# Normed frames for the gate and up projections: six of eight tiles into buffers of their own, written during the output projection

## The reference

```python
for l in range(DEPTH):                                   # DEPTH = 2
    hp = hp + mixer(rms_norm(hp, norm_mix[l]), w_in[l], ...) @ w_out[l]
    hp = hp + conv_ffn(rms_norm(hp, norm_ffn[l]), ...)

def rms_norm(x, g):
    return x * rsqrt(mean(x * x, axis=-1) + EPS) * g

def conv_ffn(h, prev, w_gate, w_up, conv_w, conv_b, w_down):
    g = h @ w_gate                                       # 1024 -> 2816
    u = h @ w_up                                         # 1024 -> 2816
    gp = concatenate([prev, g])                          # two rows of history
    gc = conv_b + sum(conv_w[i] * gp[i:i + l] for i in range(3))
    return (gelu(gc) * u) @ w_down                       # 2816 -> 1024
```

## Time and profile before

| | |
|---|---|
| median of 3 runs | 1730.74 us (1730.06 to 1736.03) |
| the profiled execution | 1730.43 us |
| its span in the trace | 1728.9 us |
| PE busy | 1640.0 us, 95% of the span |
| DVE, ACT, POOL busy | 815.6, 541.6, 374.4 us |
| mean granted TensorE clock | 0.97 of full speed |

### The profile page before, as it was taken

One profiled execution on the slowest core, in us unless ns is written; L12 is line 12 of the kernel. 1 busy time (PEld: TensorE's weight loads), 2 busy tenths in 40 slices (PEclk: granted clock), 3 DMA queues, 4 the chain that ended last, 5 costly groups with the idle time before them and its releaser, 6 DMA issues.

```text
span 1728.9 us, 30885 instructions
## 1 busy us (share of the span) xinstructions
PE 1640.0 (95%) x11500; PEld 1586.3 (92%) x11500; DVE 815.6 (47%) x1116; ACT 541.6 (31%) x829; POOL 374.4 (22%) x405
## 2 busy tenths in 40 slices
PE   5999988999999999999989998889999999999997
PEld 4999866898999999999989997579999999999997
DVE  6332378546454225553243325774554442455523
ACT  2221224514545113332132221353245531233311
POOL 5080010051222002222304501002422210122221
PEclk9999978999999999999999999799999999999998
DMA  4222343022232223322222213511223322233222
GB/s 163 68 69 74 115 171 130 2 79 85 97 121 89 97 87 104 121 70 71 81 82 65 71 61 135 211 59 38 66 87 130 120 88 73 85 122 101 69 77 85
DMA packets 44849, 160.77 MB, mean 93 GB/s; under 512 B 5952, under 2 KB 8416, under 8 KB 43936
## 3 DMA queue, kind: packets, MB, share of 16 engines
q1 hardware_dynamic: 40896, 129.11, 23.5%
q0 software_dynamic: 2464, 28.26, 4.1%
q10 hardware_dynamic: 1408, 2.30, 0.4%
HBM read 147.64 MB, written 30.88 MB: 103 GB/s over the span
## 4 chain that ended last, share of the span: by engine, by line
PE 70%; DVE 9%; issue 9%; ACT 6%; POOL 2%; DMA 2%; DVEq 1%; ACTq 1%; POOLq 0%; SPq 0%; PEldq 0%
PE PSUM L1312 55%; PE PSUM L1349 8%; PE PSUM L1298 4%; ACT WH L634 1%; PE PSUM L1340 1%; DVE CT L1230 1%; DVE CT L1233 1%; POOL YT L602 1%; ACT CT L787 1%; ACT CT L785 1%; DVE XNL L831 1%; DVE GP L1223 1%; DMA CAK<-ca_kt 1%; DVE RS L824 1%; DMA X<-x_in 1%
## 5 line engine op out<-in xcount | busy, mean ns | idle before, releaser
L1312 PE MATMUL PSUM<-XNH,WH 128*128 128x320 f32 x2400 | 557.1, 313 | 35.7 <-DVE XNL L831 32.6
L1312 PE MATMUL PSUM<-XNL,WH 128*128 128x320 f32 x2400 | 550.7, 311 | 0.0
L1312 PE MATMUL PSUM<-XNH,WL 128*128 128x320 f32 x2400 | 550.3, 310 | 0.0
L819 DVE TENSOR_TENSOR WL<-RAW,WH 128x1024 fp32r<-128x1024 f32 (+2 forms) x214 | 289.8, 1355 | 393.5 <-ACT WH L634 388.2
L1312 PEld LDWEIGHTS PSUM<-XNH,WH 128*128 128x128 f32 x2400 | 402.6, 189 | 41.7 <-DVE XNL L831 36.3
L634 ACT ACTIVATE WH<-RAW 128x1024 fp32r<-128x1024 f32 (+2 forms) x214 | 210.9, 987 | 636.3 <-PE PSUM L1312 586.0
L1312 PEld LDWEIGHTS PSUM<-XNH,WL 128*128 128x128 f32 x2400 | 404.7, 189 | 0.0
L1312 PEld LDWEIGHTS PSUM<-XNL,WH 128*128 128x128 f32 x2400 | 404.3, 189 | 0.0
L1312 PE MATMUL PSUM<-YH,WH 128*128 128x320 f32 x544 | 124.8, 311 | 5.1 <-DVE YL L1241 5.1
L1312 PE MATMUL PSUM<-YL,WH 128*128 128x320 f32 x544 | 124.6, 310 | 0.0
L1312 PE MATMUL PSUM<-YH,WL 128*128 128x320 f32 x544 | 124.5, 310 | 0.0
(11 more groups left out here) (196 smaller groups left out, 1747.3 us busy)
## 6 DMA issues: line engine op xcount, KB each, us to landing
RAW<-w_gu SPq DMA_DIRECT2D x88, 512.0 KB, 3.6
RAW<-w_in SPq DMA_DIRECT2D x46, 512.0 KB, 3.6
RAW<-w_down SPq DMA_DIRECT2D x32, 384.0 KB, 2.9
RAW<-w_down SPq DMA_DIRECT2D x32, 320.0 KB, 2.8
RAW<-w_out SPq DMA_DIRECT2D x16, 512.0 KB, 4.0
CAK<-ca_kt SPq DMA_DIRECT2D x16, 512.0 KB, 6.3
CAV<-ca_v SPq DMA_DIRECT2D x16, 512.0 KB, 4.9
ca_kt_copy<-ca_kt POOLq DMA_DIRECT2D x16, 512.0 KB, 4.8
```

What stands on the lines that cost most here:

```text
L819: nc.vector.tensor_tensor(WL[:, s, 0:width], RAW[:, s, 0:width], WH[:, s, 0:width].bitcast(F32), ALU.subtract).then_inc(lo_ready[s], 1)
L1312: last = nc.tensor.matmul(PSUM[:, b + a, 0:HALF], w[:, s, P * k:P * (k + 1)], x[:, first + k, HALF * a:HALF * (a + 1)], start=start and k ...
```

## The change

Two new buffers, `XFH` and `XFL`, of six tiles each (`EARLY` = 6) hold the high and low parts of the normed frames' tiles 0 to 5 for gate and up. They are in the scope `ffn`; by the buffers' sizes they lie over a part of `ST` and over `TAB`, `STAB`, `MS`, `CO`, `SWK`, `SWV`, `ZC` and `QKT` of the mixer. Tiles 6 and 7 stay in `XNH` and `XNL`. ScalarE writes tile m - 3 of `XFH` behind the split of unit m, for m = 3 to 8; VectorE writes tile m - 1 of `XFL` in round m, behind the split of unit m + 2, for m = 1 to 6. ScalarE first waits for `attention_stored`. Tiles 6 and 7 are written where all eight were. The first gate product waits for `residual` to reach one less, the add of m = 6. `product` and `product_by_half` take a function from the tile's number to its two operands.

```diff
+EARLY = 6
...
+            XFH = sb("XFH", [P, EARLY, FRAMES], F32R, scope=ffn)
+            XFL = sb("XFL", [P, EARLY, FRAMES], F32R, scope=ffn)
...
+        def norm_tile(name, k):
+
+            xh, xl = (XFH, XFL) if name == "ffn" and k < EARLY else (XNH, XNL)
+            return xh[:, k, :], xl[:, k, :]
+
...
-            def norm_hi(l, name, which, first_residual):
-                for k in range(KT):
+            def norm_hi(l, name, which, first_residual, tiles=range(KT)):
+                for k in tiles:
+                    xh = norm_tile(name, k)[0]
                     act.wait_ge(residual, first_residual + k + 1 - KT)
-                    normed_hi.done(nc.scalar.activation(XNH[:, k, :], X[:, k, :], ACT.Copy,
+                    normed_hi.done(nc.scalar.activation(xh, X[:, k, :], ACT.Copy,
...
+                act.wait_ge(attention_stored, 16 * STORES * (l + 1))
                 for m in range(2, KT + 1):
                     hi(l, OUT_UNIT + m)
+                    if m > 2:
+                        norm_hi(l, "ffn", 1, l * RESIDUALS + 2 * KT, [m - 3])
                 product_wait(act, l, OUT_UNIT + KT - 1)
-                norm_hi(l, "ffn", 1, l * RESIDUALS + 2 * KT)
+                norm_hi(l, "ffn", 1, l * RESIDUALS + 2 * KT, range(EARLY, KT))
                 hi(l, FFN_UNIT + 1)
...
-                    normed_lo.done(nc.vector.scalar_tensor_tensor(out=XNL[:, k, :], in0=X[:, k, :],
+                    normed_lo.done(nc.vector.scalar_tensor_tensor(out=xl, in0=X[:, k, :],
                                                                   scalar=GAIN[:, bass.ds(l, 1), which, k],
-                                                                  in1=XNH[:, k, :].bitcast(F32),
+                                                                  in1=xh.bitcast(F32),
...
                     if m < KT - 1:
                         lo(l, OUT_UNIT + m + 2)
-                norm_lo(l, "ffn", 1, l * RESIDUALS + 2 * KT)
+                    if 0 < m <= EARLY:
+                        norm_lo(l, "ffn", 1, l * RESIDUALS + 2 * KT, [m - 1])
+                norm_lo(l, "ffn", 1, l * RESIDUALS + 2 * KT, range(EARLY, KT))
                 lo(l, FFN_UNIT + 1)
...
-            def product(l, n, xh, xl, b, extra=0, tiles=KT, first=0, start=True, stop=True, ready=None):
+            def product(l, n, parts, b, extra=0, tiles=KT, first=0, start=True, stop=True, ready=None):
...
+                    xh, xl = parts(first + k)
                     for w, x in ((WH, xh), (WH, xl), (WL, xh)):
...
-                    product(l, FFN_UNIT, XNH, XNL, 0, h * FFN_EXTRA + f, ready=ready)
+                    product(l, FFN_UNIT, normed_ffn, 0, h * FFN_EXTRA + f, ready=ready)
...
-                pe.wait_ge(residual, l * RESIDUALS + 2 * KT)
+                pe.wait_ge(residual, l * RESIDUALS + 2 * KT - 1)
                 gate(0, 0, ready=lambda k: normed_lo.wait(pe, l, ("ffn", k)))
```

More of the change, by code:

```diff
@@ L824, in reciprocal_root, with norm_lo @@
                 rstd_ready.done(nc.vector.reciprocal(RS[:, :], RS[:, :]), name)
-            def norm_lo(l, name, which, first_residual):
-                for k in range(KT):
+            def norm_lo(l, name, which, first_residual, tiles=range(KT)):
+                for k in tiles:
+                    xh, xl = norm_tile(name, k)
                     dve.wait_ge(residual, first_residual + k + 1 - KT)
                     normed_hi.wait(dve, l, (name, k))
-                    normed_lo.done(nc.vector.scalar_tensor_tensor(out=XNL[:, k, :], in0=X[:, k, :],
+                    normed_lo.done(nc.vector.scalar_tensor_tensor(out=xl, in0=X[:, k, :],
                                                                   scalar=GAIN[:, bass.ds(l, 1), which, k],
-                                                                  in1=XNH[:, k, :].bitcast(F32),
+                                                                  in1=xh.bitcast(F32),
                                                                   op0=ALU.mult, op1=ALU.subtract), (name, k))
@@ L1290, in _, with product_by_half @@
         def _(pe):
-            def product_by_half(l, n, xh, xl, b, extra, tiles, first, half_done):
+            def product_by_half(l, n, parts, b, extra, tiles, first, half_done):
                 s = n % 2
@@ L1296, in product_by_half, with mixed, normed_ffn, gated @@
                     for k in range(tiles):
+                        xh, xl = parts(first + k)
                         for w, x in ((WH, xh), (WH, xl), (WL, xh)):
                             last = nc.tensor.matmul(PSUM[:, b + a, 0:HALF], w[:, s, P * k:P * (k + 1)],
-                                                    x[:, first + k, HALF * a:HALF * (a + 1)], start=False,
+                                                    x[:, HALF * a:HALF * (a + 1)], start=False,
                                                     stop=k == tiles - 1 and w is WL)
                     last.then_inc(unit_used[s] if a else half_done, 1)
-            def product(l, n, xh, xl, b, extra=0, tiles=KT, first=0, start=True, stop=True, ready=None):
+            def mixed(k):
+                return XNH[:, k, :], XNL[:, k, :]
+            def normed_ffn(k):
+                return norm_tile("ffn", k)
+            def gated(k):
+                return YH[:, k, :], YL[:, k, :]
+            def product(l, n, parts, b, extra=0, tiles=KT, first=0, start=True, stop=True, ready=None):
                 s = n % 2
@@ L1313, in product @@
                                 PSUM[:, b + a, 0:HALF], w[:, s, P * k:P * (k + 1)],
-                                x[:, first + k, HALF * a:HALF * (a + 1)],
+                                x[:, HALF * a:HALF * (a + 1)],
                                 start=start and k == 0 and w is WH and x is xh,
@@ L1536, in _ @@
                     ready = (lambda k: normed_lo.wait(pe, l, ("mix", k))) if u == 0 else None
-                    product(l, u, XNH, XNL, 2 * (u % 2), ready=ready)
+                    product(l, u, mixed, 2 * (u % 2), ready=ready)
                     if u == 0:
```

10 lines of the change are left out of this document (5 added, 5 removed).

## The result

The changed kernel took 1711.57 us (median of 4 runs, 1708.07 to 1715.93), the kernel before 1730.4 (4 runs, 1726.64 to 1736.03). The ratio is 0.989, 95% interval 0.9853 to 0.9926. The forecast was 1717.8 with a range from 1715.5 to 1722. By medians 18.8 us were gained where 12.7 were forecast; the spans of the two profiled executions differ by 1728.9 - 1711.5 = 17.4.

What follows compares the result with a forecast made beforehand. TensorE, busy 1640.0 of 1728.9 us, was taken as the bound. Removing stops and half clock before gate and up, 6.19 + 6.53 = 12.72 us, from 1730.43 gave 1717.7, stated as 1717.8, range 1715.5 to 1722.

Steps and rivals of the forecast that it cites:

- The mechanism: Between output projection and first gate product: early tiles let TensorE run on at full clock, gaining 6.19 and 6.53 us.
- the 0.9 to 2.2 us that were named: Sign in the output projection's rounds: each of VectorE's early low-part tiles takes 0.9 to 2.2 us.
- The wait for the stores: ScalarE's wait for `attention_stored` ahead of the output projection's loop: cost zero, with 96 us of slack.
- The sum: Losses from output projection to first gate product, 6.19 us in layer 0 and 6.53 in layer 1, all gained: 12.72.
- The two terms for the clock, 3.01 and 3.36: First gate product, layers 0 and 1: us lost beyond 7.04 behind the gap, at granted clock 0.50.
- No tile was late: Rival at tile 7 of the first gate product: TensorE stops, at most 1 us per layer, 1719.8 us; chance 0.07.
- The gap goes and the slow clock stays: Rival at the first gate product: half clock has another cause, only 6.35 us gained, 1724.1 us; chance 0.02.
- given back later: Rival behind the first gate product: something hangs on a fixed time, up to all lost, 1724 to 1730; chance 0.06.
- the short gaps: TensorE's gaps of 0.28 and 0.70 us behind the first gate product's column sums, predicted to stay.
- VectorE's round: Rival in the output projection: low parts over 3.73 us lengthen twelve rounds; at 6 us each, 1745 us; chance 0.03.
- the term that the sum starts from: The profiled execution of the kernel before, 1730.43 us, from which 12.72 was subtracted to give 1717.7.
- How the numbers follow: Prediction's part setting chances and range: forecast 0.82, range 1715.5 to 1722, with 2 us on its lower side.

Runs made afterwards that it cites:

- the four executions with a stop of 3.0 or 3.3: Before; before again unchanged (1729.19 us); changed kernel with all eight tiles made late (1726.97 us); changed kernel with TensorE waiting for tile 6's low part (1726.89 us).
- the other profile of before: Profile from running the kernel before once more, unchanged: 1729.19 us over 12 runs, ratio 1.0002 to before.
- three early tiles: Changed kernel with EARLY = 3 instead of 6, so tiles 3 to 7 are written behind the loop: 1721.83 us, 0.9952 of before.
- the wait for tile 6: Changed kernel, but TensorE waits for tile 6's low part before starting the first gate product: 1726.89 us, 0.999 of before.

## Why the prediction was right, and where it was wrong

**The mechanism** was right in all its steps. The rows of after show the gate pair 0.29 behind the last pair, column sums two products behind the start of m = 7, no clock under 1.00 there, 2.10 us to the reciprocal, adds 7.05 apart, and early tiles inside the 0.9 to 2.2 us that were named. The wait for the stores costs nothing: the first split behind it is still released by TensorE, as in the earlier trace rows. ScalarE's timeline of after:

```profile
338.50 1.06 ACT L642 ACTIVATE WH<-RAW 128x1024 fp32r<-128x1024 f32 x1 [6.24 <-PE PSUM L1338]
```

**The sum** for the edges, 12.72, is what the two traces show, to 0.01 us in either layer. That is closer than such a sum can be, and so in part luck: the four executions with a stop of 3.0 or 3.3 lost 5.05 to 6.56 a layer, 5.87 on average, since the half clock lasts for a varying time. A sum from the other profile of before would have said 11.6 (5.05 + 6.56). The two terms for the clock, 3.01 and 3.36, should have been given as 1.9 to 3.4 each.

**The rivals.** No tile was late; where tiles were late (three early tiles), they cost short stops as the rival said, without the clock. "The gap goes and the slow clock stays" is refuted by the wait for tile 6: the clock came back down with the stop alone. Nothing was given back later: the short gaps are as they were. VectorE's round has 1.62 us to spare. By the Trainium skill (SBUF — State Buffer, section "SBUF: two separate sides") an early tile could have been held for a whole `ACC`, 2.42 + 0.87 = 3.29 us in all as the prediction worked out; the trace has it take 2.18 and end 0.67 behind an `ACC` that had started 0.92 before it, and the next add doesn't feel it.

**The step that failed** is the range together with the term that the sum starts from. In "How the numbers follow" it says: "The range holds the forecast with 2 us on its lower side (the runs of before differ by 0.7 between the lower two)". Three runs of before were at hand, 1730.06, 1730.74 and 1736.03, and the third was left aside. And the sum, "1730.43 (profiled execution) - 12.72", takes one execution's time for everything outside the edges, as if the clock there were the same in each execution; no reason is given for that. The runs showed otherwise. The 73 executions of before have a mean of 1728.6, so that 1730.43 lies 1.8 above it, a standard deviation of 3.8 and a width of 16 us. A sum that starts from one execution and is held against the mean of four of after has a standard error of sqrt(3.8² + 4.5² / 4) = 4.4, and a median does no better. A lower side of 2.3 us could not hold that; 1.28 x 4.4 = 5.6 to each side would be 8 times in 10 for chance alone. Of the 25 executions of after 13 lie below 1715.5. What the prediction also lacked is the row that shows the cause: windows of attention in the profile of before, with a clock of 0.72 and 0.77 in stretches that the change doesn't touch, and which the profiled execution of after has at 1.00 for the same code:

```profile
290.00:300.00 10.00, 7.59 (x73) 5.66 (x62) 9.63 (x16) 4.14 (x12) 0.00 (x0) 0.72 0.01 2
300.00:310.00 10.00, 10.00 (x62) 8.60 (x61) 5.11 (x13) 4.65 (x17) 0.00 (x0) 0.77 0.00 1
```

These stretches and the fall behind the stop for `YL` are 4.7 and 1.6 us of the table.

So the forecast of the gain stands (12.7 against 13.7, between 11.7 and 15.7), and the range around the time was too narrow on its lower side by a factor of more than two. Of the 6.2 us by which the first measured time lay below the forecast, 1.8 are the start of the sum, 1.0 the gain, 0.1 rounding, and 3.3 the distance of these four runs from the mean of all 25.

## What to carry to other kernels

Cost a stop of TensorE with the clock that follows it: a stop of 3 us cost 5 to 6.6 here, one of 1.2 us cost 1.5, so 1.8 us off such a stop saved some 4 by the traces, and one late operand or one needless wait gives all of it back. Where operands share a buffer with the last reader of the stage before, buffers of their own for those needed first are enough; the last two tiles of eight could stay. Before a range is written, look for stretches far from the change in which the clock dips: they tell how much one execution can differ from the next, and a sum made against a single trace carries them.

## What the runs showed of the hardware

- The time of one program, with nothing changed, ranges over 16 us (1721.06 to 1737.29), and follows the mean granted clock at 1.3 us for 0.001.
- Whether the clock falls behind a stop is no sharp rule of its length. It stayed at 1.00 after the stops of 0.28, 0.37, 0.68, 0.95, 1.20 and 1.40 us shown above; after 2.1 to 2.25 us it fell in 10 of 20 places; after 3.0 to 3.3 us in 8 of 8, and after 5.49 in 11 of 11. What tells the 10 that fell from the 10 that didn't, and why it dips in attention in some executions, where TensorE has many short waits, no run here settles.
- At the half clock a pair of 128x320 matmuls starts every 0.54 us (22 in 5.97 us behind the wait for tile 6), at the full clock every 0.29.
- VectorE stands for 2.55 us where its loop over the layers jumps back. Written out, that is gone.
- VectorE's low part of a tile, 0.87 us alone, takes 2.18 us in all twelve early places, where GpSimd's sum of squares runs beside it.
